# Two decoder blocks and an expert layer on one core: the compression ahead of the gate chunks, the recurrent mixer in PSUM, the gate tangents within the attention

## The reference, cut to what matters

```python
# second layer
q, kc, vc, ks, vs, kw, vw, gl, z = split(h @ w_in)
kc = compress(kc, pe[0], w1[0], w2[0])   # gelu(blocks of 32 rows @ w1) @ w2, 15 blocks for each of 4 groups
vc = compress(vc, pe[1], w1[1], w2[1])
kc = rope(rms_norm(kc, k_gain[0]), cmp_pos)
o = nsa_attention(q, kc, vc, ks, vs, kw, vw, sigmoid(gl)) * silu(z)
# mixer of the third layer
xc = causal_conv(x_lru, conv_w) + conv_b                     # 4 taps
r = sigmoid(block_diag(xc, gate_a_w) + gate_a_b)
i = sigmoid(block_diag(xc, gate_x_w) + gate_x_b)
a = exp(-8 * r * softplus(-lambda))
h_t = a_t * h_(t-1) + sqrt(1 - a_t**2) * i * xc
y = concat(rms_norm(h * gelu(gate)), rms_norm(chunk_attention(q, k, v)))
```

## Time and profile before

| | us |
|---|---|
| median of 3 runs | 1825.83 (1824.26 to 1825.85) |
| the profiled execution | 1826.83, its span 1824.9 |
| TensorE busy in the span | 1598.6 (88%) |
| VectorE | 1016.2 (56%) |
| ScalarE | 817.3 (45%) |
| GpSimd | 569.6 (31%) |
| mean granted TensorE clock | 0.931 of full |

### The profile page before, as it was taken

One profiled execution on the slowest core, in us unless ns is written; L12 is line 12 of the kernel. 1 busy time (PEld: TensorE's weight loads), 2 busy tenths in 40 slices (PEclk: granted clock), 3 DMA queues, 4 the chain that ended last, 5 costly groups with the idle time before them and its releaser, 6 DMA issues.

```text
span 1824.9 us, 28509 instructions
## 1 busy us (share of the span) xinstructions
PE 1598.6 (88%) x10659; PEld 1444.9 (79%) x10659; DVE 1016.2 (56%) x2178; ACT 817.3 (45%) x1382; POOL 569.6 (31%) x212
## 2 busy tenths in 40 slices
PE   7987889869876767888799977799999999999996
PEld 6976779856675766887799966699999999999875
DVE  5724346456644574422339999655555555555554
ACT  4543325447523344333235556544444444444443
POOL 5850637730044460664467745100000000000000
PEclk9988879879988888889799989999999999999998
DMA  7630314420022221342324400355555555555453
GB/s 285 240 139 1 116 70 174 150 93 1 1 93 92 93 93 70 116 162 90 118 93 160 142 1 0 138 185 186 184 185 186 186 188 185 187 187 186 152 179 121
DMA packets 36810, 238.48 MB, mean 131 GB/s; under 512 B 4080, under 2 KB 4208, under 8 KB 12144
## 3 DMA queue, kind: packets, MB, share of 16 engines
q1 hardware_dynamic: 36720, 237.27, 36.2%
HBM read 236.21 MB, written 1.05 MB: 130 GB/s over the span
## 4 chain that ended last, share of the span: by engine, by line
PE 55%; DVE 15%; ACT 3%; issue 3%; POOL 1%; DVEq 0%; DMA 0%; ACTq 0%; POOLq 0%
PE bank L824 20%; PE bank L543 10%; PE bank L579 7%; PE bank L576 6%; PE bank L546 5%; PE bank L635 3%; DVE raw L1648 2%; DVE hThi L1237 2%; PE bank L617 2%; DVE arena L1233 1%; PE bank L804 1%; POOL wlo L863 1%; DVE arena L1528 1%; ACT whi L921 1%; DVE arena L1602 1%
## 5 line engine op out<-in xcount | busy, mean ns | idle before, releaser
L543 PE MATMUL bank<-hThi,whi 128*128 128x256 f32 x1024 | 251.7, 284 | 6.0 <-ACT whi L1130 6.0
L863 POOL TENSOR_TENSOR wlo<-arena,whi 128x2048 fp32r<-128x2048 f32 x44 | 204.5, 4648 | 152.3 <-ACT whi L921 152.3
L543 PE MATMUL bank<-hTlo,whi 128*128 128x256 f32 x1024 | 251.4, 283 | 0.0
L863 POOL TENSOR_TENSOR wlo<-raw,whi 128x2048 fp32r<-128x2048 f32 x44 | 202.8, 4613 | 110.6 <-ACT whi L921 110.6
L824 PE MATMUL bank<-whi,ghi 128*128 128x512 f32 x512 | 204.1, 399 | 1.9 <-DVE glo L1688 0.5
L543 PEld LDWEIGHTS bank<-hThi,whi 128*128 128x128 f32 x1024 | 195.8, 191 | 10.4 <-issue 6.4
L824 PE MATMUL bank<-whi,glo 128*128 128x512 f32 x512 | 202.9, 396 | 0.0
L824 PE MATMUL bank<-wlo,ghi 128*128 128x512 f32 x512 | 202.0, 395 | 0.0
L543 PEld LDWEIGHTS bank<-hTlo,whi 128*128 128x128 f32 x1024 | 196.1, 192 | 4.2 <-issue 0.2
L921 ACT ACTIVATE whi<-arena 128x2048 fp32r<-128x2048 f32 x44 | 84.3, 1916 | 229.6 <-PE bank L579 148.9
L921 ACT ACTIVATE whi<-raw 128x2048 fp32r<-128x2048 f32 x44 | 84.2, 1914 | 175.8 <-PE bank L579 111.8
(11 more groups left out here) (237 smaller groups left out, 3126.3 us busy)
## 6 DMA issues: line engine op xcount, KB each, us to landing
raw<-ex_in SPq DMA_DIRECT2D x66, 1024.0 KB, 4.8
raw<-w_in SPq DMA_DIRECT2D x44, 1024.0 KB, 4.8
arena<-w_in SPq DMA_DIRECT2D x44, 1024.0 KB, 4.8
xw<-ex_in SPq DMA_DIRECT2D x32, 1024.0 KB, 4.7
raw<-ex_in SPq DMA_DIRECT2D x50, 512.0 KB, 3.6
xw<-ex_in SPq DMA_DIRECT2D x10, 512.0 KB, 3.4
arena<-frt_in SPq DMA_DIRECT2D x1, 3904.0 KB, 15.0
arena<-tab_in SPq DMA_DIRECT2D x1, 1089.0 KB, 16.1
```

Of the source, the lines that this page charges most:

```text
L543: mm(out, lhs, rhs, start=(k == 0), stop=False)
L863: G.tensor_tensor(wlo[:, u % 2, :], slots[u % RING], whi[:, u % 2, :], ALU.subtract).then_inc(lo_ready, 1)
```

## The change

The stream in memory stays; the order of chunks in which it is run puts the two `cmp` chunks ahead of the two gate chunks, now named `nsa_z`. `cmp` units are no longer split: TensorE multiplies them straight from the ring slot in plain fp32, and SyncE refills such a slot when TensorE is through. Hidden and query transposes stand between the halves of the first gate chunk, key transposes between those of the second. The compressed key is normed with a Newton inverse root on VectorE and small operands in PSUM. Of the tangent of z the first half is one operation, the other half is four pieces at jobs 12, 18, 24 and 30 of the attention. Query and key chunks are taken as before, but chunk 4 is taken without rounding first. In the mixer lambda's softplus moves to the start of the kernel, the bias scaling behind the evictions; sigmoids become tangents in place in PSUM, the convolution and most of the recurrence take one operand from PSUM or write there, and the three reciprocals go (decay by exponential of -2 la, its factor by the same; the root multiplies (1 + tanh) and (1 + a)).

```diff
+CMP_AT = STREAM.index("cmp") - 2
+ORDER = list(range(CMP_AT)) + [CMP_AT + 2, CMP_AT + 3, CMP_AT, CMP_AT + 1] + list(range(CMP_AT + 4, NCHUNK))
+RUN = [STREAM[c] if c not in (CMP_AT, CMP_AT + 1) else "nsa_z" for c in ORDER]
+SPLIT_UNITS = [u for u in range(2 * NCHUNK) if RUN[u // 2] != "cmp"]
...
@@ SyncE, load
-                    sp_.wait_ge(lo_ready, u - RING + 1)
+                    if u - RING in SPLIT_UNITS:
+                        sp_.wait_ge(lo_ready, split_before(u - RING) + 1)
+                    else:
+                        sp_.wait_ge(proj_done, u - RING + 1)
...
@@ TensorE, second layer
             for v in range(2):
-                pe.wait_ge(ft_ready, v + 1)
+                c = first_of("cmp") + v
+                pe.wait_ge(dup_taken, 2 * GROUPS * (v + 1))
+                pe.wait_ge(takenA, taken_before(c - 1, "A"))
                 for half in range(2):
+                    u = 2 * c + half
+                    pe.wait_ge(w_loaded[u % RING], 16 * (u // RING + 1))
+                    w = slots[u % RING].rearrange("p (a n) -> p a n", a=8)
+                    for a in range(8):
+                        last = mm(bank[2 * (c % 2)][:, 0:256], FT[v][:, 8 * half + a, :], w[:, a, :],
+                                  start=(half == 0 and a == 0), stop=(half == 1 and a == 7))
                     last.then_inc(proj_done, 1)
+            pe.wait_ge(hid_gelu, 1)
+            project(first_of("nsa_z"), hidden_and_queries)
...
+            project(first_of("nsa_z") + 1, lambda: transposes("nsa_k"))
             transposes("cmp_k")
...
@@ TensorE, mixer
             for g in range(2):
+                if g == 1:
+                    pe.wait_ge(u_ready, 1)
                 for b in range(4):
+                    last = mm(high[b], bd[:, g, b, :], xc[:, b, :], start=True, stop=True)
                 last.then_inc(ri_done, 1)
                 project(c + 2 + g)
-                pe.wait_ge(ri_exp, g + 1)
...
@@ ScalarE, start
             roots(2)
+            act.wait_ge(lam_v, 1)
+            A(sp[:, 1, :], sp[:, 0, :], ACT.Exp, scale=-1.0).then_inc(lam_a, 1)
+            act.wait_ge(lam_v, 2)
+            A(sp[:, 3, :], sp[:, 2, :], ACT.Ln).then_inc(lam_a, 1)
...
@@ ScalarE, second layer
-            A(rows[:, :, 0:1024], rows[:, :, 2560:3584], ACT.Tanh, scale=0.5).then_inc(z_ready, 1)
+            hidden(0)
+            split_on(first_of("cmp"))
+            hidden(1)
+            for v in range(2):
+                act.wait_ge(hidT_done, v + 1)
+                A(hidT[v], bank[6 + v][:, 0:256], ACT.Copy).then_inc(hidT_ready, 1)
+            take(first_of("nsa_z"), scale=x_scale)
+            act.wait_ge(tr_done, tr_all("nsa_q"))
+            act.wait_ge(takenA, taken_before(first_of("nsa_z") + 1, "A"))
+            A(rows[:, :, 0:CW], rows[:, :, 2560:2560 + CW], ACT.Tanh, scale=0.5)
+            act.wait_ge(cmp_done, 1)
+            A(S[:, 0:HD], bank[6][:, 256:256 + HD], ACT.Square, accum_out=ss[:, 0:1]).then_inc(sq_ready, 1)
+            take(first_of("nsa_z") + 1, scale=x_scale)
...
@@ ScalarE, mixer
+            gate(0)
+            take(c + 2)
+            gate(1)
             act.wait_ge(u_ready, 1)
-            A(la, la, ACT.Tanh).then_inc(t_ready, 1)
+            A(lb, la, ACT.Tanh).then_inc(t_ready, 1)
+            for j in range(2):
+                last = A(low2[j], la[:, 2 * j:2 * j + 2, :], ACT.Exp, scale=-2.0)
+            last.then_inc(a_ready, 1)
+            take(c + 3)
+            act.wait_ge(ix_ready, 1)
             act.wait_ge(t_ready, 1)
-            A(lb, la, ACT.Sqrt).then_inc(t_ready, 1)
+            for j in range(2):
+                last = A(high2[j], lb[:, 2 * j:2 * j + 2, :], ACT.Sqrt)
+            last.then_inc(t_ready, 1)
             take(c + 4)
...
@@ VectorE, mixer
-                last = V.tensor_scalar(xc[:, b, :], xpad[:, b, 3:259], cw[:, b, 3:4], ...)
+                last = V.tensor_scalar(low[b], xpad[:, b, 3:259], cw[:, b, 3:4], ...)
...
+            dve.wait_ge(t_ready, 2)
+            for j in range(2):
+                last = V.scalar_tensor_tensor(ix[:, 2 * j:2 * j + 2], high2[j], 0.5, ix[:, 2 * j:2 * j + 2], ALU.mult, ALU.mult)
+            step(last)
             for b in range(4):
-                last = V.tensor_tensor_scan(lb[:, b, :], la[:, b, :], ri[:, 1, b, :], 0.0, ALU.mult, ALU.add)
+                last = V.tensor_tensor_scan(high[b], low[b], ix[:, b, :], 0.0, ALU.mult, ALU.add)
```

More of the change, by code:

```diff
@@ L290, in destinations @@
         def destinations(c):
-            s, i = STREAM[c], c - first_of(STREAM[c])
+            s, i = RUN[c], c - first_of(RUN[c])
+            if s == "nsa_z":
+                return [rows[:, t, 2560 + CW * i:2560 + CW * i + CW] for t in range(TT)]
             if s in ("moba_in", "nsa_in"):
@@ L558, in project @@
                     u = 2 * c + half
-                    pe.wait_ge(hi_ready, u + 1)
+                    if half == 1 and between is not None:
+                        between()
+                    pe.wait_ge(hi_ready, split_before(u) + 1)
                     wh, wl = (w[:, half, :].rearrange("p (k n) -> p k n", k=KT) for w in (whi, wlo))
@@ L585, in project_all @@
             def project_all(name):
-                for c in range(first_of(name), first_of(name) + STREAM.count(name)):
+                for c in range(first_of(name), first_of(name) + RUN.count(name)):
                     project(c)
@@ L926, in split_on, with take @@
                 split()
-            def take(c, func=ACT.Copy, scale=1.0):
-                if c not in ACROSS:
+            def take(c, func=ACT.Copy, scale=1.0, split_first=True):
+                if c not in ACROSS and split_first:
                     split_on(c)
@@ L953, in take_all, with last_gates @@
             def take_all(name, func=ACT.Copy, scale=1.0):
-                for c in range(first_of(name), first_of(name) + STREAM.count(name)):
+                for c in range(first_of(name), first_of(name) + RUN.count(name)):
                     take(c, func, scale)
+            def last_gates(i):
+                if i in (12, 18, 24, 30):
+                    at = CW + P * ((i - 12) // 6)
+                    last = A(rows[:, :, at:at + P], rows[:, :, 2560 + at:2560 + at + P], ACT.Tanh, scale=0.5)
+                    if i == 30:
+                        last.then_inc(z_ready, 1)
             def attention(phase):
@@ L1523, in _ @@
             for b in range(4):
[L1524 removed]
+                last = V.tensor_scalar(low[b], xpad[:, b, 3:259], cw[:, b, 3:4], sm("conv_b")[:, b:b + 1], ALU.mult, ALU.add)
             step(last)
@@ L1553, in _ @@
             dve.wait_ge(takenA, taken_before(c + 2, "A"))
-            V.tensor_tensor(la, lb, gg, ALU.mult).then_inc(rows_ready, 1)
+            for j in range(2):
+                last = V.tensor_tensor(la[:, 2 * j:2 * j + 2], high2[j], gg[:, 2 * j:2 * j + 2], ALU.mult)
+            last.then_inc(rows_ready, 1)
             take_transposed("y")
```

248 lines of the change are left out of this document (106 added, 142 removed).

## The result

The changed kernel took **1774.42 us** (median of four runs, 1772.49 to 1775.53) against 1825.76 for the one before in the same runs: a ratio of 0.972 with a 95% interval of 0.9703 to 0.9736. The profiled execution took 1775.53 us with a span of 1773.3 us, 51.6 us shorter than the span before. The forecast was 1774 us, from a sum of -52.0 us.

A forecast was written before the change was run, and what follows sets the result against it. TensorE was taken to bound the projections, starved in one stretch before the second attention and two in the mixer. +1.8 - 24.8 + 0.5 - 29.5 = -52.0 us gave 1774 us, 80% range 1765 to 1790.

The forecast's parts named there:

- Reading of the bound: TensorE bounds the projections, but not 345.2 to 391.2 us nor, in the mixer, 618.8 to 628.6 and 669.7 to 686.2.
- fp32 compression: Second layer's compression: 64 plain fp32 matmul records at 0.216 us take 13.8 us; with a cold clock 30.2 us.
- The ring (rival B): Second layer: gate units fetched with 0.8 us spare come late, three waits of 1.5 to 3 us: 1781 us; 12%.
- Key chain (rival D): Second layer: VectorE's compressed-key chain, hit by remainders, ends 10 us behind TensorE: 1784 us; 7%.
- Tangent in pieces: Half the gate tangent as four pieces of about 0.4 us in the second attention: 0.5 us more (0 to 1.6).
- Clock (rival C): Second layer's attention: TensorE granted 1.2 GHz throughout nearly doubles its 96.5 us (+88), ending slower at 1862 us; 3%.
- Lambda chain: Moved to the kernel's start, it delays a GpSimd remainder TensorE wants: 1.8 us more (0 to 2.1), not regained.
- The row norm's end: Mixer, ahead of its first projection: lambda chain gone and bias operation moved behind the evictions, 3.3 us less (2.3 to 3.9).
- Convolution in PSUM form: Mixer: sixteen operations at 0.36 us, 5.8 us in all instead of 18.9, so TensorE's 9.8 us wait goes.
- The mixer as a whole: Third attention's first exponential at 658.0 against 687.49: 29.5 us less, the 3.3 of the mixer's start among them.

The follow-up runs named there:

- the halves alone: Two runs on the kernel before: mixer and lambda parts only, 1797.65 us; second layer's part only, with the gate tangent in pieces, 1801.91 us.
- the unedited kernel: The changed kernel run again without an edit, as reference for the follow-up trials: 1774.75 us.

## Why the prediction was right

- **Reading of the bound.** Held. The two starved stretches are gone and TensorE is full in both; the halves alone give -24.7 and -29.0 us.
- **fp32 compression.** 64 records from 322.10 to 335.72, 0.213 us each, against 13.8 us said. The low end of 13.8 to 30.2 was right because the clock was at 1.00 on entry, as the earlier trace rows had it.
- **The ring (rival B).** Said: rounding at 330.4, remainder done 337.0 for a need of 337.8. Measured: rounding 330.59, remainder from 332.58, done at 337.14, TensorE at 335.72 and 337.82 without a wait. The 0.8 us of slack were 0.7 in the trace, and enough. Rival B fell.
- **Key chain (rival D).** Too slow in my working: the square on ScalarE was done at 355.0 (I said 356.9), the last of the four key evictions at 361.9 (365). I had put a table load ahead of the tangent, and there is none at 353.80; it stands ahead of Exp, at 367.00. There it is on the path, where I had nothing: ScalarE reached the attention at 367.0, 0.6 before the 367.6 said, and the 1.28 us of the load put the first Exp at 368.3, 0.7 behind it. Two errors of opposite sign nearly cancelled; that the sum was hardly hurt is luck.
- **Tangent in pieces.** +0.5 said, -0.1 in the trace; the covered end of 0 to 1.6.
- **Clock (rival C).** 0.97 granted through the second attention, 0.96 before. Fell there. But the third attention met what the rival feared, on a small scale, and the sum had no term for it. From the changed kernel, from before, and from the run with take first and late remainder:

```profile
633.50:642.00 8.50, 8.14 (x33) 6.42 (x33) 2.93 (x15) 4.80 (x21) 2.37 (x1) 0.60 0.00 1
```

```profile
687.40:695.00 7.60, 6.38 (x36) 5.06 (x37) 3.03 (x18) 5.35 (x22) 0.00 (x0) 0.89 0.01 2
```

```profile
635.00:643.00 8.00, 6.37 (x41) 5.05 (x41) 3.24 (x18) 6.51 (x26) 0.00 (x0) 1.00 0.01 3
```

From first to last Exp that attention took 17.14, 15.56 and 15.43 us. In the changed kernel it comes behind TensorE's wait of 2.2 us for the take; in the third row the take comes first and no wait of TensorE there is over 0.5 us. The length goes with the granted clock, and it came to some 1.6 us here.

- **Lambda chain.** The wait at 35.37 came as said (1.70 for 1.8). "TensorE is the bound behind, so it isn't regained" looks wrong in the table's one pair of traces, where of 1.95 us only 0.14 were left at 268, and is right over all traces, where 2.0 are kept. That the profiled pair shows less is chance. The row norm's end gained as said: first mixer matmul 593.89 to 566.42, -27.5 from -24.2 on entry, so -3.3. The forecast for the two together was -1.5; with 2.0 kept at the start it is -1.3. Of the 3.3, the trace of the run with the chain moved back gives 1.6 to the chain ahead of the row norm, as said, which leaves 1.7 for the bias operation.
- **Convolution in PSUM form.** The mechanism held, the size was low: 6.9 us for sixteen operations, 0.42 to 0.47 each, against 5.8 at 0.36 from the earlier trace rows, which were plain additions; these take a scalar per partition besides, and whether that is the reason was not tried. Ready at 589.0, needed at 591.1. The SBUF form, 1199 ns an operation beside GpSimd, cost 13.3 us. The Trainium skill (VectorE: DVE Perf Modes, Rules for kernel authors) offers a copy to SBUF ahead of many operations on matmul output. No run here has such a copy, but both forms of the convolution are there: without GpSimd beside it the SBUF form took 490 and 410 ns where the PSUM form takes 484 and 541, so the four first-tap operations lose 0.5 us in PSUM, as the prediction had worked out by that page; beside GpSimd the SBUF form took 1199 and 1365.
- **The mixer as a whole.** -29.7 for -29.5.
- **What was not foreseen** is everything behind: the third attention is 1.6 us longer by its clock, the stages between it and the experts are 2.3 shorter (the same in the unedited kernel's other trace; why was not looked into), which makes the -0.7 to -54.66, and the expert key stage took 2.8 back in this execution. I had called this part untouched. By the edit it was, but it isn't constant between executions, which alone moves the sum by nearly 3 us. That -51.6 came so near to -52.0 owes something to luck: 1.8 us of the start's loss missing, 2.3 gained unforeseen, 1.6 and 2.8 lost unforeseen.

## What to carry to other kernels

Where GpSimd streams over SBUF, price every VectorE operation beside it by the slowest of its line and not by its size, and give it a PSUM operand if a bank is free: that was worth 12 to 13 us in the convolution and 4.1 to 4.7 in eight small additions, while moving GpSimd's work elsewhere chose another victim at three places of four. Read a trial that edits two places at each of them: one that looked worthless had gained 3.5 us at one and lost 3.5 at the other. A chain of small dependent operations is best laid beside a projection of the next stage whose inputs are ready, but first ask whether its own matmuls need their splits at all: here leaving them out gave most of 18 of 24 us. A stage that a change doesn't touch can still differ by 3 us between executions, so look for the same kernel's second trace before explaining such a step, or the lack of one.

## What the hardware showed that I had not expected

- A VectorE operation on 128 x 3 numbers was held for 3.77 us, a cast of 0.43 us for 4.00 (0.99 beside GpSimd's shorter subtraction of 1.27): size is no protection from one remainder of 4.5 us.
- The hold can outlast one GpSimd instruction. One 128 x 128 addition took 8.12 us, up to GpSimd's next gap, where in another execution of the same kernel the longest was 2.57 us, about one remainder of 2.4. There is nothing between: four of twelve executions have the one, eight the other. What decides between the two was not found.
- No table load stood ahead of the gate's Tanh behind the compression's Gelu; the first Exp behind it paid 1.28 us. In the mixer it is the same (the gates' Tanh at 593.67 without a load, one of 1.28 at 609.43 ahead of Exp). Before, where a square root stood between, the load was ahead of Tanh (387.59) and Exp had none.
